# Layer 0 of a two-layer decoder trunk: the compression's inputs multiplied ahead of the convolution, with three banks exchanged

## The reference, cut to what matters

```python
z = rms_norm(h, norm_mix[layer]) @ w_in[layer]
u_ssm, z_conv, q, k_c, v_c, k_s, v_s, k_w, v_w, g_nsa = jnp.split(z, cuts, axis=-1)
y_ssm  = s5_mixer(u_ssm, ...)       # 16 groups, a 64-state complex recurrence over the 256 tokens
y_conv = conv_mixer(z_conv, ...)    # a * sigmoid(g), a causal 31-tap depthwise convolution, layer norm, silu, a product
y_nsa  = nsa_mixer(q, k_c, v_c, k_s, v_s, k_w, v_w, g_nsa, ...)
                                    # k_c, v_c: cut into overlapping blocks of 32 tokens and compressed by a small MLP
y = jnp.concatenate([_rms(y_ssm), _rms(y_conv), _rms(y_nsa)], axis=-1) * mix_out_norm[layer]
h = h + y @ w_out[layer]
h = h + cross_attention(...)
h = h + (swiglu(...) if layer % 2 == 0 else moe_swiglu(...))   # layer 0 dense, layer 1 two of 8 experts
```

## Time and profile before

| | |
|---|---|
| median of 3 runs | 1253.61 us (1252.09 to 1255.91) |
| the profiled execution, its own time | 1255.73 us |
| its span in the trace | 1253.8 us |
| around the span | 1.9 us |
| PE busy | 1224.1 us (98%) |
| DVE, ACT, POOL busy | 706.9, 423.4, 100.7 us |

### The profile page before, as it was taken

One profiled execution on the slowest core, in us unless ns is written; L12 is line 12 of the kernel. 1 busy time (PEld: TensorE's weight loads), 2 busy tenths in 40 slices (PEclk: granted clock), 3 DMA queues, 4 the chain that ended last, 5 costly groups with the idle time before them and its releaser, 6 DMA issues.

```text
span 1253.8 us, 48989 instructions
## 1 busy us (share of the span) xinstructions
PE 1224.1 (98%) x21590; PEld 1042.5 (83%) x21590; DVE 706.9 (56%) x1639; ACT 423.4 (34%) x877; POOL 100.7 (8%) x161
## 2 busy tenths in 40 slices
PE   7999999999999999999999999999999999999997
PEld 5755567788877775557799999999999999999986
DVE  6876536557866376644555555545455554554545
ACT  5516423001002142733233333333333334333332
POOL 1270110000000055011000000000000000000001
PEclk9999999999999999999999999999999999999999
DMA  9521025253451543515799999999999999999995
GB/s 373 223 93 68 1 101 217 101 202 135 168 196 74 218 188 139 206 52 193 295 418 426 424 426 425 426 427 424 426 427 427 424 427 424 427 427 424 427 423 195
DMA packets 36571, 360.97 MB, mean 288 GB/s; under 512 B 4163, under 2 KB 5827, under 8 KB 11548
## 3 DMA queue, kind: packets, MB, share of 16 engines
q1 hardware_dynamic: 33776, 354.86, 68.6%
q10 hardware_dynamic: 2156, 3.19, 0.7%
q0 software_dynamic: 576, 2.10, 0.5%
HBM read 356.77 MB, written 3.36 MB: 287 GB/s over the span
## 4 chain that ended last, share of the span: by engine, by line
PE 80%; DMA 9%; DVE 2%; SPq 1%; ACT 1%; issue 0%; POOL 0%; DVEq 0%; ACTq 0%
PE bank L2609 25%; PE bank L1951 18%; PE bank L2626 12%; DMA ring<-moe_w_dram 9%; PE bank L2554 6%; PE bank L2323 4%; PE bank L2311 2%; PE bank L1959 2%; PE bank L2595 2%; PE bank L2252 1%; PE bank L2340 1%; SPq L548 1%; PE bank L2645 1%; PE bank L2132 1%; PE bank L2059 0%
## 5 line engine op out<-in xcount | busy, mean ns | idle before, releaser
L2609 PE MATMUL bank<-R,ring 128*64 128x80 f32 x11264 | 427.3, 233 | 7.6 <-DVE ring L1840 5.5
L2609 PEld LDWEIGHTS bank<-R,ring 128*64 128x64 f32 x11264 | 404.6, 137 | 15.4 <-DVE ring L1840 13.0
L1951 PE MATMUL bank<-ring 128*128 128x128 f32 (+2 forms) x1760 | 284.5, 321 | 1.6 <-ACT ring L668 0.9
L1951 PEld LDWEIGHTS bank<-ring 128*128 128x128 f32 x1760 | 239.9, 191 | 49.1 <-issue 36.6
L2626 PE MATMUL bank<-zz,ring 128*64 128x80 f32 x5632 | 224.7, 233 | 0.0
L1013 ACT ACTIVATE ring<-ring 128x1024 f32<-128x1024 f32 x160 | 169.1, 1057 | 134.4 <-PE bank L2626 134.4
L2626 PEld LDWEIGHTS bank<-zz,ring 128*64 128x64 f32 x5632 | 207.9, 137 | 0.0
L1891 DVE SCALAR_TENSOR_TENSOR zz<-zz,bank 128x80 f32<-128x80 f32 x176 | 41.9, 238 | 162.8 <-PE bank L2609 161.7
L1840 DVE COPY ring<-ring 128x1024 f32<-128x1024 f32 x160 | 110.0, 688 | 27.7 <-DMA ring<-moe_w_dram 27.4
L1018 ACT ACTIVATE sqx<-bank 128x80 f32<-128x80 f32 x176 | 41.7, 237 | 222.4 <-PE bank L2609 221.8
L1844 DVE COPY ring<-ring 128x1024 f32<-128x1024 f32 x160 | 109.8, 686 | 0.2 <-DVE R L1830 0.2
(11 more groups left out here) (352 smaller groups left out, 1118.0 us busy)
## 6 DMA issues: line engine op xcount, KB each, us to landing
ring<-moe_w_dram SPq DMA_DIRECT2D x158, 1536.0 KB, 22.3
ring<-ffn_w_dram SPq DMA_DIRECT2D x11, 3072.0 KB, 10.1
ring<-w_in_dram SPq DMA_DIRECT2D x6, 2048.0 KB, 7.2
extra<-moe_w_dram SPq DMA_DIRECT2D x8, 1536.0 KB, 23.7
ring<-w_out_dram SPq DMA_DIRECT2D x4, 2048.0 KB, 8.1
ring<-w_small_dram SPq DMA_DIRECT2D x2, 3072.0 KB, 10.2
ring<-w_x_dram SPq DMA_DIRECT2D x2, 3072.0 KB, 11.0
ring<-w_in_dram SPq DMA_DIRECT2D x2, 2144.0 KB, 15.1
```

What stands on the lines that cost most here:

```text
L1951: i = pe.matmul(out_ap, a, b, start=(k == 0), stop=(k == n - 1))
L2609: e = pe.matmul(pb[out_bank][c0:c0 + 64, 0:CAP], half[:, P * k + c0:P * k + c0 + 64], xg[:, k], start=(k == 0), stop=(k == KT - 1), tile_p ...
```

## The change

Only layer 0 is changed. On PE the list of projections now has `kvc_half(0)`, `kvc_half(1)` and then `conv`. The table `S5_AT` is as before, so that `bu((6, 7))` still stands behind position 9 and `ys(0)` behind position 10; position 9 is now `kvc_half(1)` and position 10 is `conv`. Three contents change banks: `kvc` goes from bank 1 to 6, `conv` from 6 to 7, and tile 6 of S5 from 7 to 1. On ACT the four copies of `kvc` stand ahead of the two of `conv`. Layer 1 has its old order and banks.

```diff
         for j, bank in enumerate(BU_BANKS):
-            a(f"bu{j}_", bank)
+            a(f"bu{j}_", 1 if j == 6 and l == 0 else bank)
         a("ys", 2)
-        a("conv", 6)
-        a("q0_", 5, 2); a("q1_", 0, 2); a("kvc", 1); a("kv0_", 6, 3); a("kv1_", 7, 3); a("gates", 1)
+        if l == 0:
+            a("kvc", 6); a("conv", 7)
+        else:
+            a("conv", 6)
+        a("q0_", 5, 2); a("q1_", 0, 2); 
+        if l:
+            a("kvc", 1)
+        a("kv0_", 6, 3); a("kv1_", 7, 3); a("gates", 1)
...
+                if l == 0:
+                    kvc_copy()
+                    conv_copy()
+                else:
+                    conv_copy()
+                    kvc_copy()
...
-                               conv, lambda: kvc_half(0), lambda: kvc_half(1), lambda: kv_tile(0), lambda: kv_tile(1), lambda: ys(1), gate_logits]
+                               *([lambda: kvc_half(0), lambda: kvc_half(1), conv] if l == 0 else
+                                 [conv, lambda: kvc_half(0), lambda: kvc_half(1)]), lambda: kv_tile(0), lambda: kv_tile(1), lambda: ys(1), gate_logits]
```

More of the change, by code:

```diff
@@ L783, in _, with conv_copy, kvc_copy @@
                     act.activation(sq[:], ps(f"q{i}_{l}")[:], ACT.Square).then_inc(banks.drain(f"q{i}_{l}"), 1)
[L784 to L795, removed]
+                def conv_copy():
+                    nm = f"conv{l}"
+                    banks.wait(act, nm)
+                    for a in range(2):
+                        k = act.activation(ca[:, a], ps(nm)[:, 256 * a:256 * a + 256], ACT.Identity, scale=0.5,
+                                           bias=par[:, G_CB + 2 * l + a:G_CB + 2 * l + a + 1])
+                    k.then_inc(banks.drain(nm), 1)
+                def kvc_copy():
+                    banks.wait(act, f"kvc{l}")
+                    kvc = ps(f"kvc{l}")[:].rearrange("p (v t) -> p v t", v=2)
+                    act.activation(CX[0:64, :, 0, 0:240], kvc[0:64, :, 0:240], ACT.Copy)
+                    act.activation(CX[0:64, :, 1, 0:240], kvc[64:128, :, 0:240], ACT.Copy)
+                    act.activation(CX[64:128, :, 0, 0:240], kvc[0:64, :, 16:256], ACT.Copy)
+                    act.activation(CX[64:128, :, 1, 0:240], kvc[64:128, :, 16:256], ACT.Copy).then_inc(banks.drain(f"kvc{l}"), 1)
+                if l == 0:
[4 more added lines that the diff above has]
+                    kvc_copy()
                 weights_in(act, f"small_{l}")
```

## The result

The changed kernel takes 1257.2 us (median of 20 executions, 1255.1 to 1260.08) against 1252.97 us of the kernel before in the same comparison (20 executions, 1251.74 to 1257.76). The ratio is 1.0031, with a 95% interval of 1.0024 to 1.0039: slower by 3.0 to 4.9 us. The forecast was 1258.3 us within 1254.8 to 1261.3. The profiled execution took 1257.01 us, its span is 1255.2 us, 1.4 us longer than the span of before.

What follows compares the result with a forecast made beforehand. The prediction took PE to set the end. Against the median of 1253.61 us, 4.70 - 1.88 = 2.82 us for the order plus 1.9 us for the clock gave +4.7 us, 1258.3 us, range 1254.8 to 1261.3.

Steps and rivals of the forecast that it cites:

- Removed: Layer 0, PE ahead of the convolution: the wait for DVE's diagonal table goes, 1.88 us gained.
- the banks are free: Layer 0: the three exchanged banks cost nothing; bank 6 is free 3.5 us before `kv_tile(0)` needs it.
- Added: Layer 0, PE ahead of `bu((6, 7))`: a new 4.70 us wait for DVE to drain tile 4 from bank 3.
- The clock: PE's standstill in layer 0 drops the granted clock to 1.2 GHz, costing 1.9 us, bounds zero and 3.6 us.
- the row at the router: Profile row of a clock fall, 611.0 to 614.4 us; 64 matmuls took 4.03 against 2.21 us, priced at 1.8 us.
- The sum: Whole kernel: 2.82 us net of the order plus 1.9 us of the clock, 4.7 us slower.
- The wait alone: Rival: the clock stays at 2.4 GHz through PE's layer 0 wait; +2.8 us, 1256.4 us; chance 0.20.
- Absorbed in the experts: Rival: the experts' weight stream sets the end and PE's 4.7 us vanish; 1253.6 us; chance 0.07.
- The change does what it says: Rival: only the table's 1.88 us go and no wait replaces them; 1251.7 us; chance 0.03.
- The longer low clock: Layer 0: the clock's fall costs 3.6 us; +6.4 us, 1260.0 us; within the forecast's 0.70 for either length.
- the first part: Opening on what bounds the kernel: a microsecond PE wins or loses here reaches the end unless something further on absorbs it.

Runs made afterwards that it cites:

- the banks alone: Changed kernel's three exchanged banks and ACT order, with PE's old order, against the kernel before: 0.9999 [0.9987, 1.0011].
- filler: Changed kernel plus 9 matmuls of constants (about 4 us) ahead of S5's tiles 6 and 7, against the kernel before: 1.0022 and 1.0009 in two runs.
- tiles 6 and 7 last: Changed kernel with S5's tiles 6 and 7 behind the convolution in layer 0, against the kernel before: 0.9993 [0.9982, 1.0004].
- first dose: Kernel before plus 20 matmuls of constants (8.64 us) ahead of S5's first output in layer 0: 1.0050, 6.3 us slower.
- both layers: Layer 0's best version plus, in layer 1, gates ahead of S5's second output and DVE's keys first, against the kernel before: 0.9996 [0.9981, 1.0011].
- tiles 6 and 7 early in the old order: Kernel before with S5's tiles 6 and 7 ahead of the compression's first half in layer 0: 1.0023 [1.0010, 1.0036].
- both doses: Kernel before plus 20, then 60 matmuls of constants ahead of S5's first output in layer 0: 1.0050 and 1.0197.
- the version for layer 0: Also the best version: changed kernel, tiles 6 and 7 behind the convolution, kv banks swapped, ACT, gates and DVE keys reordered; against before 0.9990 and 0.9988.

## Why the prediction was right, and where a term was off

**Removed.** The table's wait of 1.88 us: gone in all profiles of the changed kernel. That ACT's copying first is worth nothing, and that the banks are free, held: in the run of the banks alone and by ACT's rows.

**Added.** 4.70 us of wait were forecast. 4.76 us were measured where the program started as in the profile of before, 4.10 us in the two executions that started faster. The term hangs on how far DVE is ahead of PE: in the first profile of after the table was begun 0.14 us ahead of tiles 4 and 5, in that of before 0.50 us behind them. The table's wait shrinks by as much with it, so the net of the order is the same for both starts: 2.74, 2.75 and 2.74 us in the stretch, compared with a before that started alike. Forecast 2.82. The filler runs, which have the order without the fall, measured 1.1 to 2.8 us in the time.

**The clock.** The fall came, three times of three. Its cost in the stretch was sized at 1.9 us, after the row at the router; it is 2.60, 3.02 and 2.70 us. This is the term that the sum had too small, by about 1 us. The low level lasted 6.8 us each time instead of the router's 3.4, and 5.7 us or more of these had work in them. The row was one draw: in other profiles the low level at the router lasted 6.8 us (tiles 6 and 7 last, first dose) and 10.2 us (both layers). The price was also a little too high: the 64 entries of 4.03 us and the 64 of 2.21 us have one form but are not the same work, and the former took 2.39 us where the clock stayed up, so that fall cost 1.64 us and not 1.8. The forecast's upper bound of 3.6 us covered the measured cost.

**The sum.** 4.7 us forecast; 5.34, 5.77 and 5.44 us in the stretch; 3.0 to 4.9 us in the time. So the sum was too small for the stretch, and about 2 us of what the stretch shows do not reach the time (1.4 us by the ratio of the first comparison, 2.4 and 2.0 us by those of the others). That a delay reaches the end in full was the second flaw. The two errors, a clock term about 1 us too small and an arrival about 2 us too high, partly cancel: that 4.7 lies so near the measured 3.9 us is in part luck. The mechanism is not.

Where the 2 us go is not shown. The mean granted clocks give a lead: they are 0.9960 over the 44 executions of the changed kernel and 0.9964 over the 90 of before, although a fall of 6.8 us alone takes 0.0027 of the span. So the changed kernel should have less low clock elsewhere. (These means also hold some low clock behind PE's last matmul, from about 1249 us on, which costs PE nothing.) In the profiles the other place within the work is the router: of the nine of kernels without a fall or filler in layer 0's stretch the clock fell there in six (before, tiles 6 and 7 last, tiles 6 and 7 early in the old order, both doses, the version for both layers) and not in three (the banks alone, the version for layer 0 twice); it fell in none of the three of the changed kernel, nor in the two with the filler. And it costs time: of the 90 executions of before the 18 with a mean clock of 0.998 or more took 1251.9 us in the mean, the other 72 took 1253.8 us. If most executions of before pay for a fall at the router and most of the changed kernel do not, some 1.3 to 1.6 us of the 2 are explained; this is an estimate, from four fifths of 1.64 us (one fall in the chain) or of 1.95 us (the difference of these means). Why the fall becomes rarer is open. Arriving later can't be the whole reason: of the filler's executions 17 of 23 have 0.998 or more, of the doses' 10 of 12, but of those with tiles 6 and 7 early, delayed by as much as the filler's, 1 of 8, and of the best version's, which arrive earlier than before, 11 of 24.

**Rivals.** The wait alone: excluded by the profiles; its size is what the filler shows. Absorbed in the experts: excluded as a whole by both doses and by the measured loss; a fixed amount of 1 to 2 us is not excluded, only unexplained. The change does what it says: this was decided by DVE's drain, which ended at 66.2 to 68.5 us, as written. The longer low clock was the best of the sizes. One statement of the first part was too broad: that a microsecond won by PE in this stretch reaches the end. It was not put into the sum. The run with tiles 6 and 7 last shows that POOL's last states and ACT's copies stood ready to take all of it, which the rows told: PE came to `ys(1)` 0.06 us behind POOL.

## What to carry to other kernels

Moving a piece ahead to fill a gap uncovers what that piece used to hide: list for every piece that is passed over or now comes earlier which buffer it opens and when the last reader leaves it, here 0.76 us ahead of need before the change and 4.70 us behind it after. A stall of several microseconds on PE has a second price in the clock, which can be told from the first by putting harmless matmuls into the wait. Compare such stretches only between executions that started alike. And a gap is only worth what the next engine leaves of it, so look how close the other chains arrive at the next meeting point before filling it.

## What the runs showed of the hardware

- A standstill of PE of 1.81 us and one of 2.87 us left the granted clock at 1.00; those of 4.10, 4.76 and 4.10 us brought it to 0.50 for 6.8 us each, 0.3 to 1.1 us ahead of PE's return.
- The start of the program has two paces. In five of the fourteen profiles PE reached S5's tiles 4 and 5 at 53.8 to 54.1 us, in the other nine at 55.4 to 55.8 us, for the same instructions, so that two profiles may differ by 1.6 us before the change is reached. The difference arises in PE's first work, which the timelines of before and of after show in the same sixteen entries:

```profile
12.12 3.67 PE L1994 MATMUL bank<-cst,xn 128*128 128x128 f32 x16
11.37 1.97 PE L2010 MATMUL bank<-cst,xn 128*128 128x128 f32 x16
```

They take 1.97 us in the five and 3.57 or 3.67 us in the nine. That this is TensorE's clock rising earlier or later is argued from the ratio; the granted clock reads 1.00 in both. Single profiled spans are no measure of a change of this size; distances within them are, between executions that started alike.
